# Hybrid attention, mLSTM and experts block: rotary tables awaited in the second projection pass, first tile normalised and transposed in the modulation stage, query columns of the mixer weights loaded last

## The reference

```python
mod_x = silu(c) @ w_mod + b_mod            # six vectors of 1024: sh1, sc1, g1, sh2, sc2, g2
mod_c = silu(c_ctx) @ w_mod + b_mod        # the same six for the context
hx = rms_norm(x, norm1_g) * (1 + sc1) + sh1
hc = rms_norm(ctx, norm1_g) * (1 + csc1) + csh1
px, pc = hx @ w_in, hc @ w_in              # columns: latents for attention (672), mLSTM query (256),
                                           # key (256), value (512), output gate (512), gates (16)
x = x + g1 * (attention and mLSTM of px, pc) @ w_out
x = x + g2 * routed_ffn(rms_norm(x, norm2_g) * (1 + sc2) + sh2)     # top 4 of 32 experts
return rms_norm(x, final_norm_g)
```

## Time and profile before

| what | value |
|---|---|
| median of three runs | 2754.6 us |
| lowest and highest of them | 2749.3 and 2755.75 us |
| device time of the profiled execution | 2749.94 us |
| its span | 2748.1 us |
| PE busy | 2597.6 us, 95% of the span |
| modulation stage, from the start to the first instruction behind it | 40.36 us |
| first matmul of the first projection pass | 47.77 us |

### The profile page before, as it was taken

How to read it: one execution, slowest core, us unless ns; L and a number is a source line. 1 busy time by engine, 2 the same in 40 slices (tenths; PEclk the granted TensorE clock), 3 DMA queues, 4 the chain that set the end, 5 groups by cost and what they waited for, 6 DMA issues and landing times.

```text
span 2748.1 us, 37447 instructions
## 1 busy us (share of the span) xinstructions
PE 2597.6 (95%) x12444; PEld 1930.6 (70%) x12444; DVE 2150.8 (78%) x2101; ACT 1596.1 (58%) x1633; POOL 564.8 (21%) x471
## 2 busy tenths in 40 slices
PE   5999998999989589999999999999999999999994
PEld 2775564555557478888888888888888888888873
DVE  1114356676747689999999999999999999999996
ACT  1221233544542167777777777777777777777775
POOL 0000031655663012111111111111111111111122
PEclk8999999999989789999999999999999999999997
DMA  7530031000123635542965999587569666959994
GB/s 269 199 116 0 25 88 65 7 7 3 34 59 118 229 121 197 193 157 58 362 207 193 376 377 377 193 315 257 198 206 369 213 214 214 316 193 378 376 345 147
DMA packets 228571, 533.92 MB, mean 194 GB/s; under 512 B 26753, under 2 KB 29218, under 8 KB 227394
## 3 DMA queue, kind: packets, MB, share of 16 engines
q1 hardware_dynamic: 211712, 481.95, 48.1%
q0 software_dynamic: 13968, 50.86, 7.8%
q10 hardware_dynamic: 2834, 0.36, 0.1%
HBM read 494.22 MB, written 38.90 MB: 194 GB/s over the span
## 4 chain that ended last, share of the span: by engine, by line
PE 61%; DMA 1%; issue 1%; DVE 1%; POOL 0%; ACT 0%; POOLq 0%; ACTq 0%; DVEq 0%; SPq 0%
PE PS L1927 56%; PE PS L1920 3%; PE PS L1937 2%; DMA acc_dram<-y,idxs 1%; DMA rows<-acc_dram 0%; DVE wl L2086 0%; DMA xg<-h_dram,idxg 0%; POOL var L1905 0%; DVE xTl L2079 0%; ACT sqj L2057 0%; DVE y L2134 0%; POOL rt L1907 0%; POOL idxs L1886 0%; ACT wh L2013 0%; DVE hid L2108 0%
## 5 line engine op out<-in xcount | busy, mean ns | idle before, releaser
L2086 DVE TENSOR_TENSOR wl<-w,wh 128x2048 fp32r<-128x2048 f32 x580 | 1301.9, 2285 | 27.3 <-ACT wh L2013 21.3
L2013 ACT ACTIVATE wh<-w 128x2048 fp32r<-128x2048 f32 x580 | 1111.3, 1916 | 306.4 <-PE PS L1927 291.8
L1927 PE MATMUL PS<-wh,xTh 128*128 128x512 f32 x1536 | 497.8, 405 | 2.0 <-DVE xTl L2079 2.0
L1927 PE MATMUL PS<-wl,xTh 128*128 128x512 f32 x1536 | 475.3, 391 | 0.0
L1927 PE MATMUL PS<-wh,xTl 128*128 128x512 f32 x1536 | 474.4, 390 | 0.0
L1894 POOL DMA_INDIRECT acc_dram<-y,idxs x48 | 144.6, 3013 | 1081.6 <-DVE y L2134 1058.1
L1927 PEld LDWEIGHTS PS<-wh,xTh 128*128 128x128 f32 x1536 | 285.9, 189 | 66.3 <-DVE wl L2086 2.9
L1927 PEld LDWEIGHTS PS<-wl,xTh 128*128 128x128 f32 x1536 | 288.9, 188 | 61.9
L1927 PEld LDWEIGHTS PS<-wh,xTl 128*128 128x128 f32 x1536 | 288.9, 188 | 61.7
L1927 PE MATMUL PS<-wh,hTh 128*128 128x512 f32 x768 | 261.6, 422 | 0.0
L1927 PE MATMUL PS<-wh,hTl 128*128 128x512 f32 x768 | 241.0, 395 | 0.0
(11 more groups left out here) (347 smaller groups left out, 3035.6 us busy)
## 6 DMA issues: line engine op xcount, KB each, us to landing
w<-in_w_gu_dram SPq DMA_DIRECT2D x512, 512.0 KB, 8.3
w<-in_w_down_dram SPq DMA_DIRECT2D x128, 1024.0 KB, 10.6
later_wmod<-in_w_mod_dram SPq DMA_DIRECT2D x8, 2048.0 KB, 7.9
wmod<-in_w_mod_dram SPq DMA_DIRECT2D x8, 1024.0 KB, 13.5
w_mixer<-in_w_in_dram SPq DMA_DIRECT2D x8, 512.0 KB, 19.5
x<-in_x_dram SPq DMA_DIRECT2D x8, 512.0 KB, 3.5
rowm<-rowm_dram SPq DMA_DIRECT2D x16, 256.0 KB, 3.3
w_out<-in_w_out_dram SPq DMA_DIRECT2D x1, 4096.0 KB, 12.8
```

What stands on the lines that cost most here:

```text
L1927: mm = pe.matmul(PS[:, bank + g, :], op[:, k, :], ws[slot][:, kk, g, :], start=False, stop=(last and op is xs[1]))
L2013: act.activation(wh[c % SLOTS][:, :], w[c][:, :], ACT.Copy).then_inc(s_hi, 1)
L2086: dve.tensor_tensor(wl[c % SLOTS][:, :], w[c % NW][:, :], wh[c % SLOTS][:, :].bitcast(F32), ALU.subtract).then_inc(s_lo, 1)
```

## The change

In the modulation stage SP now issues the first context tile ahead of `w_mod`, and the second one in the middle of the mixer weights. The eight blocks of mixer weights leave out their first 256 columns (rows of 3 KB in place of 4 KB). Behind the gate columns a new load brings these 256 query columns for all eight blocks at once (1024 rows of 1 KB), with a semaphore of its own; PE waits for it in the projection stage ahead of the first latent tile. SP no longer waits for the rotary tables and the biases; DVE waits for them at the end of its first pass. ACT loads its table of functions ahead of its loads, and behind the exponential it takes the statistics of the first context tile. DVE normalises that tile, and PE transposes it behind the fifth of the eight blocks of `w_mod`. The projection stage starts with the scaled copies of that tile (`hx_copy(0)`).

```diff
@@ phase_modulation
-        m.s_wA = [sem(f"mixer_weights_in{k}") for k in range(KD + 1)]
+        m.s_wA = [sem(f"mixer_weights_in{k}") for k in range(KD + 2)]
+        m.s_ld, m.s_xn0, m.s_xT0 = s_ld, sem("xn_of_tile0_ready"), sem("tile0_in_psum")
+        s_st = sem("tile0_statistics")
...
             @block.sync
...
+                sp.dma_start(m.x0[:, :], csrc[0]).then_inc(m.s_x[0], 16)
                 for k in range(KD):
                     sp.dma_start(wch[k][:, :], wsrc[k][:, 0:WIDE]).then_inc(s_w[k], 16)
-                for t in range(TC):
-                    sp.dma_start((m.x0, m.x1)[t][:, :], csrc[t]).then_inc(m.s_x[t], 16)
                 for k in range(KD):
-                    sp.dma_start(m.wA[:, k, 0:1024], w_in_src[k][:, C_MQ:C_O]).then_inc(m.s_wA[k], 16)
-                sp.dma_start(m.wA[:, :, 1024:1040], a["w_in"].rearrange("l (k p) n -> p (l k) n", p=P)[:, :, C_G:]).then_inc(m.s_wA[KD], 16)
-                sp.wait_ge(s_ld, 16 * 3)
+                    sp.dma_start(m.wA[:, k, 256:1024], w_in_src[k][:, C_MQ + 256:C_O]).then_inc(m.s_wA[k], 16)
+                    if k == KD // 2:
+                        sp.dma_start(m.x1[:, :], csrc[1]).then_inc(m.s_x[1], 16)
+                w_all = a["w_in"].rearrange("l (k p) n -> p (l k) n", p=P)
+                sp.dma_start(m.wA[:, :, 1024:1040], w_all[:, :, C_G:]).then_inc(m.s_wA[KD], 16)
+                sp.dma_start(m.wA[:, :, 0:256], w_all[:, :, C_MQ:C_MQ + 256]).then_inc(m.s_wA[KD + 1], 16)
...
             @block.vector
...
                 chain.done(dve.tensor_copy(m.cols[:, :], PS[:, 3, 0:N_COLS]))
+                dve.wait_ge(s_st, 3)
+                dve.tensor_scalar(m.xn0[:, :], m.x0[:, :], st[:, 4:5], None, ALU.mult).then_inc(m.s_xn0, 1)
                 dve.wait_ge(s_mm, 1)
...
             @block.tensor
...
+                    if k == KD // 2:
+                        pe.wait_ge(m.s_xn0, 1)
+                        for c in range(KD):
+                            tr = pe.transpose(PS[:, 6 + c // 4, (c % 4) * P:(c % 4 + 1) * P], m.xn0[:, c * P:(c + 1) * P], m.ident[:, :])
+                        tr.then_inc(m.s_xT0, 1)
...
             @block.scalar
...
+                act.preload_act_table_set("natural_log_exp_and_others")
...
                 act.activation(cexp[:, :], PS[:, 2, 0:16], ACT.Exp, scale=-1.0).then_inc(s_exp, 1)
+                act.wait_ge(m.s_x[0], 16)
+                act.activation(junk[:, :], m.x0[:, :], ACT.Square, accum_out=st[:, 0:1]).then_inc(s_st, 1)
+                act.wait_ge(s_st, 1)
+                act.activation(st[:, 3:4], st[:, 0:1], ACT.Ln, bias=m.eps[:, 0:1], scale=1.0 / D).then_inc(s_st, 1)
+                act.wait_ge(s_st, 2)
+                act.activation(st[:, 4:5], st[:, 3:4], ACT.Exp, scale=-0.5).then_inc(s_st, 1)
@@ phase_projection
-                    sp.wait_ge(s_xn, t - 1)
+                    sp.wait_ge(m.s_xn0, 1) if t == TC else sp.wait_ge(s_xn, t - 1)
...
-                act.preload_act_table_set("natural_log_exp_and_others")
-                x_stats(0)
+                act.sem_inc(s_rstd, 1)
                 hx_copy(0)
...
-                x_norm(0)
+                dve.sem_inc(s_xn, 1)
                 hx_copy(0)
...
                 gd = Chain(dve, s_gd)
+                dve.wait_ge(m.s_ld, 16 * 3)
...
-                x_transposes(0)
+                pe.sem_inc(s_xT, 1)
                 for t in range(NT):
...
+                        else:
+                            pe.wait_ge(m.s_wA[KD + 1], 16)
```

More of the change, by code:

```diff
@@ L107, in phase_modulation @@
         m.s_x = [sem("xtile_in0"), sem("xtile_in1")]
-        m.s_wA = [sem(f"mixer_weights_in{k}") for k in range(KD + 1)]
+        m.s_wA = [sem(f"mixer_weights_in{k}") for k in range(KD + 2)]
+        m.s_ld, m.s_xn0, m.s_xT0 = s_ld, sem("xn_of_tile0_ready"), sem("tile0_in_psum")
+        s_st = sem("tile0_statistics")
         (m.x0, m.x1), _ = m.run(m.R1 + 32768 + 4 * KEYS + 8192, [("x0", [P, D], F32), ("x1", [P, D], F32)])
+        m.xn0 = m.at("xn0", [P, D], F32, m.R1 + 7 * 4096)
+        junk, st = m.at("junk0", [P, D], BF16, m.R1 + 32768 + 4 * KEYS + 16384), m.at("stats0", [P, 16], F32, m.R1 + 6 * 4096)
         with nc.Block() as block:
@@ L351, in x_stats @@
                     act.wait_ge(m.s_x[t % 2], 16 * (t // 2) + 16)
-                    if t:
+                    if t > 1:
                         act.wait_ge(s_xn, t)
@@ L357, in hx_copy @@
                 def hx_copy(t):
-                    act.wait_ge(s_xT, t + 1)
+                    act.wait_ge(s_xT, t + 1) if t else act.wait_ge(m.s_xT0, 1)
                     sc, sh = (m.s1c, R_CSH1) if t < TC else (m.s1x, R_SH1)
@@ L426, in hx_copy @@
                 def hx_copy(t):
-                    dve.wait_ge(s_xT, t + 1)
+                    dve.wait_ge(s_xT, t + 1) if t else dve.wait_ge(m.s_xT0, 1)
                     sc, sh = (m.s1c, R_CSH1) if t < TC else (m.s1x, R_SH1)
```

## The result

Median of six executions of each: 2752.21 us before (2748.82 to 2756.91) and 2740.44 us after (2739.32 to 2744.13), a ratio of 0.996 with a 95% interval of 0.9948 to 0.9973. The medians lie 11.8 us apart; the forecast was a gain of 10.7 us and 2743.9 us. A second set of five executions of the changed kernel gave 2738.16 us against 2750.58 us, ratio 0.9958 (0.9945 to 0.9972), so 12.4 us.

What follows compares the result with a forecast made beforehand. The pass was taken as PE's own work, so an earlier first matmul gains directly: -5.4 (SP's wait) - 5.9 (first tile) + 0.6 (clock) = -10.7 us, from 2754.6 to 2743.9 us; range 2737 to 2750.

Steps and rivals of the forecast that it cites:

- SP's issuing holds the stage: Modulation stage's end: without the wait, SP's blocked last issue ends at 34.5 us; projection starts at 34.95, not 40.36: -5.4 us.
- DVE's end: End of the modulation stage: DVE's chain ends at 31.0 us, ahead of SP, so it does not set the stage's end.
- The first tile: Projection start: all but the copies move ahead, leaving 1.55 us of 7.41 before the first matmul: -5.9 us.
- Arrivals: Loads for the projection stage: mixer blocks, gate columns, query columns and first latent tile come in time; no PE wait before 120 us.
- rival C: Query columns crawl on SP's queue and land at 70 us; PE stands from 62; gain 2.7 us, slower if later; chance 0.04.
- rival B: Stage end waits for the query columns' landing at 42 to 43 us; gain 2 to 3 us; 0.15 for both kinds.
- B's milder kind: Query columns must be wholly in the queue; SP ends near 38 us, gain 7 us, 2747.5; within the 0.15 for both kinds.
- Rival A: Small-row issue doesn't block SP; DVE's end at 31.0 us sets the stage, first matmul at 33.0, time 2740.4; chance 0.12.
- The clock: First mixer group: without transposes directly ahead, TensorE's full clock comes after some 4.8 us, not 3.58: +0.6 us (0 to 1.2).
- upper value of 5.97 us: Modulation stage: the matmul pace doubles only after 5.97 us; the 4.8 us expected in the first group lies between 3.58 and this.
- The sum: Whole kernel: -5.4 - 5.9 + 0.6 = -10.7 us, first matmul at 36.5 us, time 2743.9 us, -0.39%.
- a shrinking distance: Later stages: the traces should stay a constant 10 to 11 us apart; the prediction is wrong if this distance shrinks.

Runs made afterwards that it cites:

- gates first: Changed kernel with the gate columns' load moved behind the first context tile, ahead of `w_mod`; 2738.26 us, ratio 0.9955.
- no split: Changed kernel with 4 KB mixer rows of all 1024 columns and no load of its own for the query columns; 2737.15 us, ratio 0.9953.
- the second half of the query columns: From the changed kernel with the query columns in two loads of 512 rows in place of one of 1,024; 2738.72 us in a single execution.
- the late tile: Kernel without the split, with the first context tile's load behind `w_mod` and its work at the modulation stage's end; 2735.20 us, ratio 0.9947.

## Why the prediction was right

**SP's issuing holds the stage.** Forecast: SP's end at 34.5 us, stage start at 34.95. Measured: 33.38 and 33.78. That SP's issuing is what holds the stage was right and is shown by three kernels: with the hold taken away (issue in the next stage, gates first, no split) DVE's end sets the stage's. The size was off by 1.1 us, and SP's end lies just outside the forecast's own bounds of 33.5 to 36.7, since the packets ahead at the end of the issue were 1,420, not 1,226 to 1,316. The rate was right: the 3 KB rows and the second tile went at 498 packets in the 4 us from 30 to 34, or 125 per us, inside the bounds of 106 and 140. The term of -5.4 us measured -6.6. The rule behind it, that an issue ends at one fixed count of packets ahead, is not a rule: the second half of the query columns was let through at 1,821. Why it came so near in the changed kernel stays open.

**DVE's end** was forecast at 31.0 us and measured at 31.86, because the last block of `w_mod` ran at half the clock, 1.93 us in place of 1.06. It came before SP's end all the same. In the kernels without SP's hold it is what bounds the stage.

**The first tile.** -5.9 us forecast, 7.41 - 1.66 = 5.75 measured. Its new place cost PE nothing: the transposes took 1.09 us at 21.04, the next block of `w_mod` followed at 22.06 without a gap, and for the one after it, at 24.59, PE still had to wait 1.47 us.

**Arrivals.** PE had no wait on a load between the stage's start and 120 us. The query columns landed at 25.63 + 16.7 = 42.3 us, against a need at 60.6:

```profile
w_mixer<-in_w_in_dram SPq DMA_DIRECT2D x1, 1024.0 KB, 16.7
```

That rules out rival C, and with a stage start at 33.78 us, long before this landing, rival B as well: leaving this block didn't wait for the transfer. B's milder kind, in which SP ends near 38 us, falls with SP's end at 33.38 us. Rival A had the effect right for other kernels: an unheld SP gives the first matmul at 33.3 to 34.5 us (forecast 33.0).

**The clock.** +0.6 us forecast. The full clock came 4.6 us into the first group, where 4.8 were expected. The group took 44.68 - 35.44 = 9.24 us in place of 56.56 - 47.77 = 8.79, so +0.45. The number is good, its reason is not shown. The forecast took it that transposes directly ahead of the group bring the rise forward. With them the clock rose 3.7 us into the group in the kernel before and 4.0 us with SP's wait alone removed; without them it rose at 3.3 and 5.8 us in the two profiles of the kernel without the split, at 4.6 and 5.4 us in those of the changed kernel, and at 4.1 to 6.1 us in the others but the late tile (all read in windows of 0.1 us). So one kernel has values on both sides of 3.7 and 4.0, and a single trace from each side can't show the effect of the transposes. It was in part luck that the term came out. The forecast's upper value of 5.97 us is weak too: it is read from the pace of the matmuls, while the clock column of the same row says 1.00. The Trainium skill ("TensorE: Matmul & The Clock Gate", Part 1) says that activity releases the throttle. The traces agree this far: in each of the thirteen the clock rose while PE was at work, or within 0.1 us of it. How soon it rises they do not tie to the transposes; the late tile, with the whole group at 1.00, fits such a tie in one execution.

**The sum.** -6.58 - 5.75 + 0.45 = -11.9 us in the traces, the medians 11.8. The forecast of 10.7 was short by the size of SP's hold. The forecast also named a shrinking distance as a sign of being wrong. It did shrink in the first profile, from 11.9 to 5.8 us, and did not in the second, 11.8 us at the end.

**What the forecast did not see** is how the gain divides. It booked 5.4 us on the wait and 5.9 on the tile. The wait alone gives 8.95 and the rest alone 7.88 us of the first matmul's lead. With the rest in place, removing the wait is worth 39.89 - 35.44 = 4.45 us only, since the tables land sooner and SP's and DVE's work end later than without it. The split, which the forecast left unpriced by itself, costs 1.3 us.

## What to carry to other kernels

A load that must be waited for at the end of a stage should be waited for where it is read: one line moved gave about three quarters of this lead (8.95 of 12.33 us). A queue's issues are work of the engine that issues them, and at a stage's end they hold everybody; here a load of 1,024 rows near the end of the list made the next issue wait 7.75 us. Its place ahead of the large loads took that hold away but delayed them by 1.3 us; issuing the last load in the next stage took it away for nothing. When several edits bear on the same stage, cost each with the other in place, and try each alone before booking both.

## What the runs showed of the hardware

An issue behind a load of 1,024 rows took 7.75 us, until 1,420 packets were left ahead of it, and 0.84 us where that load was long gone. All held issues but one ended at 1,393 to 1,429 packets ahead of them. The rows' size had no part in it: 1,024 rows of 64 bytes and of 1 KB ahead held the next issue for 7.75 and 7.77 us, and 512 rows for 3.65 and 4.10 us. One case, 512 rows of 1 KB behind 1,024 of 64 bytes, did not hold the next issue (0.80 us, with 1,821 packets ahead), and is not explained. The small rows on ACT's queue and the larger ones on SP's went through one to one: 500 to 498 packets from 30 to 34 us in the changed kernel with rows of 3 KB, 421 to 423 in the kernel without the split with rows of 4 KB. The tables landed at 37.8 us in the first and at 41.6 us in the second. The clock's rise after the start of the first group varied between two executions of one kernel by 2.5 us (3.3 and 5.8 us).
